# A two-layer streaming encoder on one core: where the latents' norms are taken

## The reference

```python
h = rmsnorm(x, norm_g) * (1.0 + scale) + shift
z = h @ w_in                      # 1024 -> 2752 columns, split into twelve parts; m_q (256), m_kv (128), m_kr (64) are latents
cq = rmsnorm(m_q, q_norm_g)       # over 256
qm = cq @ w_uq                    # 4 heads, 128 + 64 (rotary)
ckv = rmsnorm(m_kv, kv_norm_g)    # over 128; also an output
kv = ckv_all @ w_ukv
s = (q_nope . k_nope + q_rope . k_rope) * 192 ** -0.5
p = softmax(s); out = p @ v       # gated, beside a convolution and a local attention
x = x + gate * (concat(...) @ w_out)
```

## Time and profile before

| | |
|---|---|
| median of 3 runs | 1199.44 us (1198.84 to 1199.67) |
| profiled execution, its own time | 1198.91 us |
| its span | 1197.1 us |
| TensorE busy | 1153.7 us |
| VectorE / ScalarE / GpSimd busy | 621.9 / 444.9 / 72.0 us |
| granted TensorE clock, mean | 0.993 |

### The profile page before, as it was taken

One profiled execution on the slowest core, in us unless ns is written; L12 is line 12 of the kernel. 1 busy time (PEld: TensorE's weight loads), 2 busy tenths in 40 slices (PEclk: granted clock), 3 DMA queues, 4 the chain that ended last, 5 costly groups with the idle time before them and its releaser, 6 DMA issues.

```text
span 1197.1 us, 17950 instructions
## 1 busy us (share of the span) xinstructions
PE 1153.7 (96%) x7238; PEld 1032.3 (86%) x7238; DVE 621.9 (52%) x1065; ACT 444.9 (37%) x789; POOL 72.0 (6%) x49
## 2 busy tenths in 40 slices
PE   4899999999999999999999999999999999999996
PEld 3689999999996667689999999999999757769996
DVE  5852333336448866663385233243554887666135
ACT  3552321222246544451265223122223845445122
POOL 2200001000000000002130000100000000000211
PEclk9899999999999999999999999999999999999998
DMA  9621120111123443283131211111103261106003
GB/s 331 249 75 35 35 71 17 44 52 42 49 81 129 162 143 116 71 289 144 47 113 39 75 35 35 51 36 36 58 10 105 81 220 52 45 15 249 1 28 132
DMA packets 71869, 107.72 MB, mean 90 GB/s; under 512 B 3952, under 2 KB 59376, under 8 KB 70512
## 3 DMA queue, kind: packets, MB, share of 16 engines
q1 hardware_dynamic: 71792, 106.67, 26.5%
HBM read 93.91 MB, written 11.70 MB: 88 GB/s over the span
## 4 chain that ended last, share of the span: by engine, by line
PE 88%; DVE 6%; ACT 4%; DMA 1%; issue 1%; SPq 0%; POOLq 0%; POOL 0%; ACTq 0%; DVEq 0%
PE psum L930 56%; PE psum L1303 6%; PE psum L1357 5%; PE psum L1337 3%; PE psum L921 1%; DVE h_lo L1865 1%; ACT rot L1517 1%; PE psum L1376 1%; PE psum L1256 1%; PE psum L1293 1%; DVE w_lo L1979 1%; DMA x<-in_xT 1%; PE psum L1292 1%; PE psum L1141 1%; PE psum L1313 1%; PE psum L1318 1%
## 5 line engine op out<-in xcount | busy, mean ns | idle before, releaser
L930 PE MATMUL psum<-h_hi,w_hi 128*128 128x384 f32 x1392 | 473.8, 340 | 11.3 <-DVE h_lo L1923 5.6
L930 PE MATMUL psum<-h_hi,w_lo 128*128 128x384 f32 x1392 | 465.8, 335 | 0.0
L930 PE MATMUL psum<-h_lo,w_hi 128*128 128x384 f32 x1392 | 465.8, 335 | 0.0
L930 PEld LDWEIGHTS psum<-h_hi,w_hi 128*128 128x128 f32 x1392 | 261.8, 188 | 19.6 <-issue 9.2
L930 PEld LDWEIGHTS psum<-h_hi,w_lo 128*128 128x128 f32 x1392 | 262.0, 188 | 0.5 <-issue 0.5
L930 PEld LDWEIGHTS psum<-h_lo,w_hi 128*128 128x128 f32 x1392 | 261.7, 188 | 0.0
L1979 DVE TENSOR_TENSOR w_lo<-raw,w_hi 128x1024 fp32r<-128x1024 f32 x61 | 77.3, 1268 | 201.6 <-ACT w_hi L1512 200.9
L1512 ACT ACTIVATE w_hi<-raw 128x1024 fp32r<-128x1024 f32 (+1 forms) x62 | 65.3, 1053 | 250.9 <-PE psum L930 170.9
L1357 PE MATMUL psum<-pT,ckv 128*128 128x512 f32 x144 | 74.0, 599 | 0.8 <-ACT oL_s L1650 0.8
L1577 ACT ACTIVATE probs_p<-psum,nmax 128x128 f32<-128x128 f32 (+1 forms) x72 | 25.1, 361 | 120.9 <-DVE esink L1979 120.9
L765 POOL TENSOR_TENSOR sq_a<-sq_a,sq_a 128x768 f32<-128x768 f32 x12 | 22.1, 1843 | 750.9 <-ACT sq_a L1455 750.9
(11 more groups left out here) (243 smaller groups left out, 1463.8 us busy)
## 6 DMA issues: line engine op xcount, KB each, us to landing
raw<-in_w_in SPq DMA_DIRECT2D x18, 1024.0 KB, 5.4
raw<-in_w_mod SPq DMA_DIRECT2D x15, 1024.0 KB, 5.2
modw<-in_w_mod SPq DMA_DIRECT2D x8, 1024.0 KB, 14.3
raw<-in_w_out SPq DMA_DIRECT2D x10, 768.0 KB, 5.1
tab<-in_c_rope SPq DMA_DIRECT2D x6, 1152.0 KB, 5.2
x<-in_xT SPq DMA_DIRECT2D x3, 1536.0 KB, 9.6
x<-in_xT SPq DMA_DIRECT2D x2, 2304.0 KB, 10.8
x<-x_scratch SPq DMA_DIRECT2D x2, 2304.0 KB, 10.4
```

What stands on the lines that cost most here:

```text
L930: mm = pe.matmul(psum[:, bank, 0:BLK], w_[:, k, :], h[:, k, blk(n)], start=(k == 0 and i == 0), stop=(k == KD - 1 and i == 2))
```

## The change

The key-value latents' norm is taken with tokens on partitions. VectorE copies chunk 0 raw to `ckvT`; ScalarE no longer squares it. In chunk 10 TensorE turns the nine tiles (`raw_turn`), ScalarE copies them to `lat_t` and squares them with a running sum straight into `meanl`. VectorE multiplies `lat_t` by the factors, spread along the free dimension; TensorE turns it back in chunk 11 (`turn_latents`), and ScalarE's copy to `ckvT` applies `kv_norm_g`.

The sums of the query squares come from transposes too (`squares_turn`), reduced by VectorE along the free dimension. For the prompt the queries' factor isn't applied to `cq`: it goes into `q_scale`, one column per query tile, which the exponential and `nmax` take in place of the constant. For the samples' 128 columns of `cq` it is spread (`sample_query_spread`) and multiplied as before.

```diff
-ACT_CHUNKS = [c for c in range(NIN) if c // 2 in (KV_KR, Q_LAT, S_Q, S_G, M_G0, M_G1, CV_G) or c == 2 * SK_SV]
+ACT_CHUNKS = [c for c in range(NIN) if c // 2 in (KV_KR, Q_LAT, S_Q, S_G, M_G0, M_G1, CV_G) and c or c == 2 * SK_SV]
+Q_SQUARED = ACT_CHUNKS.index(2 * Q_LAT + 1) + 1
...
+    lat_t = at("lat_t", G_AT, [P, TILES, P])
+    lat_junk = at("lat_junk", G_AT + 4 * 4 * NTOK, [P, TILES, P])
...
+    q_scale = sm("q_scale", [P, 2, TILES])
...
@@ SyncE, before the states are stored
-                sp.wait_ge(lat_ok.sem, lat_ok.at(lane.layer, 2 * NBLK))
+                sp.wait_ge(lat_c.sem, lat_c.at(lane.layer, 3))
...
@@ GpSimd
-                pool.wait_ge(z_act.sem, z_act.at(lane.layer, 2 * Q_LAT + 2))
+                pool.wait_ge(z_act.sem, z_act.at(lane.layer, Q_SQUARED))
...
@@ TensorE: latent_sums and latent_spread go
+                def raw_turn(n):
+                    if n:
+                        pe.wait_ge(raw_c.sem, raw_c.at(lane.layer, n))
+                    else:
                         pe.wait_ge(lo_h.sem, lo_h.at(lane.layer, 2))
+                    for i in range(4 if n < 2 else 1):
+                        mm = pe.transpose(psum[:, 6, tile(i)], ckvT[:, tile(4 * n + i)], ident[:])
+                    mm.then_inc(raw_T.sem, 1)
+                def squares_turn(n):
+                    if n == 2:
+                        pe.wait_ge(lat_acc.sem, lat_acc.at(lane.layer, 1))
+                        pe.wait_ge(raw_c.sem, raw_c.at(lane.layer, 2))
+                    elif n == 0:
+                        pe.wait_ge(raw_c.sem, raw_c.at(lane.layer, 3))
+                        pe.wait_ge(qsq_r.sem, qsq_r.at(lane.layer, 1))
                     else:
+                        pe.wait_ge(svt_c.sem, svt_c.at(lane.layer, 3))
+                    for i in range(4) if n < 2 else (1,):
+                        mm = pe.transpose(psum[:, 6 + n % 2, tile(i)], mix[:, 1, tile(4 * n + i if n < 2 else ST)], ident[:])
+                    mm.then_inc(qsq_T.sem, 1)
+                def turn_latents(n):
+                    if n == 0:
+                        pe.wait_ge(lat_n.sem, lat_n.at(lane.layer, 1))
+                    if n < 2:
+                        pe.wait_ge(qsq_r.sem, qsq_r.at(lane.layer, n + 2))
+                    else:
+                        pe.wait_ge(lat_c.sem, lat_c.at(lane.layer, 1))
+                    for i in range(4 if n < 2 else 1):
+                        mm = pe.transpose(psum[:, 6 + n % 2, tile(i)], lat_t[:, 4 * n + i, :], ident[:])
+                    mm.then_inc(lat_T.sem, 1)
+                def sample_query_spread():
+                    pe.wait_ge(lat_rstd.sem, lat_rstd.at(lane.layer, 2))
+                    pe.wait_ge(lat_c.sem, lat_c.at(lane.layer, 2))
+                    pe.matmul(psum[:, 7, 0:P], rstdl[:, 1, ST:TILES].broadcast_to([P, P]), ident[:], start=True, stop=True)\
+                        .then_inc(q_bc.sem, 1)
...
@@ TensorE, after block n of chunk 10 (s == 0) and chunk 11
                         if s == 0:
-                            if n < 2:
-                                latent_sums(n)
+                            if n == 2:
+                                squares_turn(2)
+                            raw_turn(n)
                             turn_values(n)
+                        elif n == 0:
+                            squares_turn(0)
+                            squares_turn(1)
+                        elif n == 1:
+                            turn_latents(0)
+                            turn_latents(1)
                         else:
-                            latent_spread(2 * n)
-                            latent_spread(2 * n + 1)
+                            turn_latents(2)
+                            sample_query_spread()
...
@@ ScalarE, after chunk 9 and after chunk 10
                         for n in range(3):
+                            w = 4 if n < 2 else 1
+                            act.wait_ge(raw_T.sem, raw_T.at(lane.layer, n + 1))
+                            lane.link(act.activation(lat_t[:, 4 * n:4 * n + w, :],
+                                                     psum[:, 6, 0:P * w].rearrange("p (t c) -> p t c", c=P), ACT.Copy),
+                                      raw_c)
                             act.wait_ge(svt_T.sem, svt_T.at(lane.layer, n + 1))
...
+                            for t in range(4 * n, 4 * n + w):
+                                ins = act.activation(lat_junk[:, t, :], lat_t[:, t, :], ACT.Square,
+                                                     accum_out=meanl[:, 0, t:t + 1])
+                            lane.link(ins, lat_sq if n == 2 else None)
+                    if c == 2 * SPLIT_AFTER:
+                        for n in range(3):
+                            act.wait_ge(lat_T.sem, lat_T.at(lane.layer, n + 1))
+                            cols = slice(4 * P * n, min(4 * P * (n + 1), NTOK))
+                            lane.link(act.activation(ckvT[:, cols], psum[:, 6 + n % 2, 0:cols.stop - cols.start], ACT.Copy,
+                                                     scale=vec[:, V_KVG:V_KVG + 1]), lat_c)
...
@@ ScalarE, exponential of a job
-                    lane.link(act.activation(p_view(j), s_view(j), ACT.Exp, bias=nmax[:, s, 0:1], scale=MLA_SCALE,
+                    g = GROUP_OF[j]
+                    scale = q_scale[:, 0, g["idx"]:g["idx"] + 1] if g["kind"] == "mla_p" else MLA_SCALE
+                    lane.link(act.activation(p_view(j), s_view(j), ACT.Exp, bias=nmax[:, s, 0:1], scale=scale,
...
@@ VectorE, chunk 0, after chunk 9, after chunk 10
-                        ts(b3(ckvT[:]), z, vec[:, V_KVG:V_KVG + 1], None, ALU.mult, sig=z_dve)
+                        cp(b3(ckvT[:]), z, sig=z_dve)
...
+                        dve.wait_ge(lat_sq.sem, lat_sq.at(lane.layer, 1))
+                        ts(meanl[:, 0, :], meanl[:, 0, :], 1.0 / 128, EPS, ALU.mult, ALU.add, sig=lat_mean)
                     if c == 2 * SPLIT_AFTER:
...
+                        for i, n in enumerate((2, 0, 1)):
+                            dve.wait_ge(qsq_T.sem, qsq_T.at(lane.layer, i + 1))
+                            if n == 2:
+                                dve.wait_ge(raw_c.sem, raw_c.at(lane.layer, 3))
+                            a, w = (P, 1) if n == 2 else (0, 4)
+                            lane.link(dve.tensor_reduce(meanl[:, 1, 4 * n:4 * n + w],
+                                                        psum[:, 6 + n % 2, a:a + P * w].rearrange("p (t c) -> p t c", c=P),
+                                                        AX.X, ALU.add), qsq_r)
+                            if n == 2:
+                                dve.wait_ge(lat_rstd.sem, lat_rstd.at(lane.layer, 1))
+                                tt(lat_t[:], lat_t[:], spread(rstdl[:, 0, :], P), ALU.mult, sig=lat_n)
+                        ts(meanl[:, 1, :], meanl[:, 1, :], 1.0 / 256, EPS, ALU.mult, ALU.add, sig=lat_mean)
+                        dve.wait_ge(lat_rstd.sem, lat_rstd.at(lane.layer, 2))
+                        for a, sign in enumerate((1, -1)):
+                            ts(q_scale[:, a, :], rstdl[:, 1, :], sign * MLA_SCALE, None, ALU.mult)
+                        dve.wait_ge(q_bc.sem, q_bc.at(lane.layer, 1))
+                        tt(cq[:, :, SEQ:NTOK], cq[:, :, SEQ:NTOK], psum[:, 7, 0:P].unsqueeze(1).broadcast_to([P, 2, P]),
+                           ALU.mult, sig=q_ok)
...
@@ VectorE, maximum of a job
-                    ts(nmax[:, s, 0:1], smax[:, s, 0:1], -MLA_SCALE, None, ALU.mult, sig=negmax)
+                    g = GROUP_OF[j]
+                    scale = q_scale[:, 1, g["idx"]:g["idx"] + 1] if g["kind"] == "mla_p" else -MLA_SCALE
+                    ts(nmax[:, s, 0:1], smax[:, s, 0:1], scale, None, ALU.mult, sig=negmax)
```

More of the change, by code:

```diff
@@ L405, in build @@
     kr_rot = sg("key_rope_rotated", 1)
-    lat_sum = sg("latents_summed", 1)
+    raw_T = sg("raw_latents_turned", 3)
+    raw_c = sg("raw_latents_copied", 3)
+    lat_sq = sg("latent_squares_summed", 1)
+    qsq_T = sg("query_squares_turned", 3)
+    qsq_r = sg("query_squares_summed", 3)
     lat_mean = sg("latent_means_ready", 2)
     lat_rstd = sg("latent_rstds_ready", 2)
-    lat_bc = sg("latent_rstds_spread", 2 * NBLK)
-    lat_ok = sg("latents_normed", 2 * NBLK)
+    lat_n = sg("turned_latents_normed", 1)
+    lat_T = sg("latents_turned_back", 3)
+    lat_c = sg("latents_normed", 3)
+    q_bc = sg("sample_query_rstds_spread", 1)
+    q_ok = sg("sample_queries_normed", 1)
     svt_T = sg("swa_values_turned", 3)
@@ L1084, in turn_values @@
                     mm.then_inc(svt_T.sem, 1)
[L1086 to L1100, removed]
                 for c in (2 * SPLIT_AFTER, 2 * SPLIT_AFTER + 1):
@@ L1123, in local_scores @@
                         pe.wait_ge(roped.sem, roped.at(lane.layer, 4))
-                        pe.wait_ge(lat_ok.sem, lat_ok.at(lane.layer, 2 * NBLK))
+                        pe.wait_ge(lat_c.sem, lat_c.at(lane.layer, 3))
```

(17 more changed lines are left out.)

20 lines of the change are left out of this document (3 added, 17 removed).

## The result

The changed kernel took 1192.46 us, the median of 4 runs (1192.08 to 1193.92), beside 1199.38 us for the kernel before in 4 runs. The ratio is 0.9945 with a 95% interval of 0.9934 to 0.9957, that is 5.2 to 7.9 us faster. Its profiled execution is the highest of its four: 1193.92 us, span 1192.1.

What follows compares the result with a forecast made beforehand. TensorE, busy 96% of the span, was taken as the bound. Per layer -7.82 + 3.49 + 1.13 - 0.06 + 0.3 = -2.96, for two layers -5.9, so 1193.5 us (-0.5%); own range 1191.5 to 1195.5, 8-in-10 range 1190.5 to 1196.8.

Steps and rivals of the forecast that it cites:

- gone from TensorE: Per layer, two `latent_sums` groups (3.80 us) and three `latent_spread` pairs (4.02 us) leave TensorE: -7.82 us.
- transposes and `sample_query_spread`: Per layer, 27 transposes (3.27 us) and one two-pass product (0.22) come to TensorE: +3.49 us, low end 3.2.
- new wait: After block 0 of chunk 11, `squares_turn(0)` waits for VectorE's first reduction: +1.13 us a layer, between 0.8 and 1.5.
- chunk 0's copy: On chunk 0's path a scaled copy (1.418 us) becomes a plain one (1.357): -0.06 us a layer.
- attention: Exponentials and `nmax` take scale columns, 9.6 us of engine time, mostly under TensorE: +0.3 us a layer, bounds 0 and 4.8.
- The stretch: Chunks 10 and 11 take 30.7 us from the end of chunk 9's products in place of 33.9.
- 0.1 for a cold first instruction: At `squares_turn(0)`, 0.1 us added to the 1.03 us TensorE stands waiting, making +1.13 a layer.
- VectorE's chain `w_hi`, `w_lo`, `ckvT` stays: At chunk 0, removing ScalarE's square (1.13 us) shortens no wait, since `w_lo` ended later (69.83 against 69.72).
- No wait: Rival in chunk 11: short ScalarE and VectorE instructions run faster, 2 x 1.13 us less, 1191.2 us; chance 0.08.
- Attention on the path: Rival: all 0.15 us of the 64 attention jobs land on the path, 9.6 us, giving 1202.5 us; chance 0.12.
- Transposes at 0.275 us: Rival: 27 new transposes cost full duration, 7.4 us, so +1.2 a layer and 1201.8 us; chance 0.04.
- A second wait of 1 us: Rival in the latents' statistics stretch: another wait of about 1 us, giving 1195.5 us; chance 0.04.

Runs made afterwards that it cites:

- experiment 1: Kernel before, with only the exponentials' and `nmax` scale taken from a column holding the old constant: 1198.64 us, ratio 0.9999.
- experiment 2: Changed kernel, with VectorE's first reduction of query squares moved ahead of `w_lo` and the gate product: 1190.05 us, ratio 0.9924.
- experiment 5: Changed kernel, with VectorE's copy of latent chunk 0 moved ahead of `w_lo` of chunk 2: 1190.03 us, ratio 0.9923.
- experiment 3: Changed kernel, with each of the 27 new transposes a layer issued twice: 1199.45 us, ratio 1.0003.
- 8: Changed kernel, with VectorE's copy of chunk 0 ahead of `w_lo`, and ScalarE's square of chunk 0 put back: 1196.4 us, ratio 0.9981.
- 4: Kernel before, with the queries' factors in the exponential's scale and spread for the samples only; sums and key-value latents as before: 1195.99 us, ratio 0.9973.
- 6: Changed kernel, with both VectorE moves, samples' reduction first and copy of latent chunk 0 first: 1186.93 us, ratio 0.9899.
- 7: Changed kernel, with ScalarE's square of chunk 0 put back, its result unused, and the copy waiting for it: 1193.54 us, ratio 0.9953.

## Why the prediction was right

The forecast was 1193.5 us, 1191.5 to 1195.5 as its own range; the median is 1192.46. Its mechanism was the one that happened, and the terms stand as follows, per layer.

| term | forecast | measured |
|---|---|---|
| gone from TensorE | -7.82 | all gone; 72 instructions |
| transposes and `sample_query_spread` | +3.49 (low end 3.2) | +3.37: `raw_turn` 0.44 + 0.44 + 0.12, `squares_turn` 0.11 + 1.06, `turn_latents` 0.87 + 0.11, spread 0.22 |
| new wait | +1.13 | +1.1 |
| chunk 0's copy | -0.06 | 1.43 to 1.37 us, -0.06 |
| attention | +0.3 | +0.28 and +0.22 in the two layers; +0.21 and +0.20 in experiment 1 |

- **The stretch.** Its terms give -3.20 for chunks 10 and 11; -3.45 was measured. From the end of chunk 9 (about 172.7) to chunk 12 it is 30.5 us where 30.7 was forecast. The groups of four came at 0.44 and not at 0.49: the low end that the prediction kept was the better value (-0.12 with what stands beside it in the table). The two old groups of `turn_values` also went from 0.49 to 0.44, which no term had (-0.10), and the wait was 0.03 shorter: together the 0.25.
- **The wait.** The steps came as written: from the end t of chunk 10 (186.96) the forecast was `w_hi` at t + 1.39, `w_lo` at 2.54, the reduction's end at 5.47, TensorE at 5.54; they are at 1.37, 2.52, 5.47 and 5.61. That the wait sat at this line and no other was right too: neither `turn_latents` nor `sample_query_spread` waits. The 0.1 for a cold first instruction came from no row; the wait itself was 1.1 where 1.03 was worked out, and the eight transposes behind it took 0.19 longer than eight elsewhere.
- **What the prediction didn't ask** was whether the wait had to be there. The instruction behind which it forms was put last of three on VectorE, and its inputs are ready by about t + 0.6 (the transpose at 187.07, the last copy at 187.57); experiment 2 moved it and gained 2.4 us. Likewise it held that with the square gone "VectorE's chain `w_hi`, `w_lo`, `ckvT` stays": true for the diff, but the removal had taken away what made the copy wait, and experiment 5 collects 2.4 us from that.
- **The rivals.** No wait: the waits of the trace and experiment 2 decide against it. Attention on the path: experiment 1, with 0.4 us of 9.6 by the traces, and at one place a layer, not at four to six. Transposes at 0.275 us: experiment 3. A second wait of 1 us: not in the list of TensorE's waits.
- **What remains.** By medians 1.0 us more was gained than the forecast had. By the two traces, without the 0.30 and the 1.55 that are not of the change, it is 6.2 where the terms give 5.9: 0.5 more by the two stretches, 0.1 more by the attention, and 0.3 less by small shifts between and behind them that no term has. The other 0.7 lies between traces and medians. The kernel before was seen in two groups of runs, five of 39 at 1197.6 to 1197.9 (mean clock 0.994) and the others at 1198.7 to 1199.9, and the changed kernel has three of its four at 0.994. How much of the 6.9 is such a difference between executions isn't settled; with so few runs that the median came so near is in part luck.

## What to carry to other kernels

Price a small operation on a full TensorE by the spacing of its instructions in the chain: a transpose in one instruction cost 0.11 us here and a product in two passes 0.21 to 0.22, though a transpose's record lasts 0.28. When an edit adds a wait, read what stands ahead of the awaited instruction on its own engine, and when it removes a reader, read which orders that reader had made right: two such moves gained nearly as much here (5.5 us) as the change itself (6.9). Added time on engines that stand idle beside the busy one costs little: of 9.6 us the traces show 0.4 on the path.

## What the runs showed of the hardware that was not expected

Behind TensorE's wait at chunk 2 of layer 0 (1.9 us) the granted clock sometimes falls to its lower level, 1.2 GHz in place of 2.4. Windows of 2 us, first of the changed kernel, then of the kernel before (busy of each engine and the clock, columns as in the earlier trace rows):

```profile
70.00:72.00 2.00, 0.94 (x5) 0.97 (x6) 1.97 (x2) 1.94 (x3) 0.00 (x0) 1.00 0.00 0
72.00:74.00 2.00, 2.00 (x9) 2.00 (x9) 1.30 (x2) 0.67 (x1) 0.00 (x0) 0.63 0.33 35
74.00:76.00 2.00, 2.00 (x8) 2.00 (x8) 0.23 (x1) 1.65 (x2) 0.00 (x0) 0.52 1.00 346
```

```profile
70.00:72.00 2.00, 0.58 (x3) 0.61 (x4) 1.97 (x2) 1.94 (x2) 0.00 (x0) 1.00 0.00 0
72.00:74.00 2.00, 2.00 (x14) 2.00 (x13) 1.21 (x2) 1.13 (x1) 0.00 (x0) 1.00 0.17 16
```

TensorE is as busy in both (2.00 of 2.00 from 72 on), but the windows at the lower level hold 9 and 8 matmuls, the one at the upper level 14. The loss is 2 x (0.37 + 0.48) = 1.7 us by the windows; by the chain it is 1.55, from the end of the wait to the end of chunk 10's block 0.

The same fall, at the same place, is in the profiled executions of experiments 2, 3 and 8, and in none of 1, 4, 5, 6 and 7. In 5 and 6 the wait ahead of it is 0.6 us. In the others it is 1.8 us or more, with the fall (the changed kernel, 2, 3, 8) and without it (the kernel before, 1, 4, 7). So the length of the wait alone doesn't decide; that it is a matter of the single execution is likely, but no kernel has two traces. Nor is it shown that the shorter wait of experiments 5 and 6 spares them: one trace each, and a kernel with the wait lengthened step by step was not run.

The mean clock of a run doesn't tell whether it had the fall. Every trace also has a stretch at the lower level at the start of the work on layer 0 and one at the end, and they are not equally long: from 36 to 42 us in windows of 2 us the changed kernel shows 0.50, 0.50 and 0.55, experiment 2 0.87, 0.50 and 0.78. So experiment 2's profiled execution has the fall, is the highest of its five (1191.17 us), and has a mean of 0.994, like the runs of other kernels that seem free of it. What follows for measuring: on this kernel 1.5 us between two runs can be this alone, so differences under about 2 us want several runs, and the traces of both kernels compared stage by stage.
